# Routed experts as passes of four 32-column strips, 96 places an expert

## What is computed

```python
def moe(h, router_w, router_b, w1, w3, w2):          # h: 384 tokens x 1024
    scores = sigmoid(t @ router_w)                   # 16 experts in 4 groups
    ...                                              # best group, then its two best experts
    combine = sum(one_hot(e_idx, 16) * wts[..., None], axis=1)
    hid = silu(einsum('td,edf->tef', t, w1)) * einsum('td,edf->tef', t, w3)   # f = 256
    hid = hid * combine[:, :, None]
    return einsum('tef,efd->td', hid, w2)
```

## Time and profile before

| | |
|---|---|
| median of 3 runs | 921.61 us (921.53 to 923.45) |
| span of the profiled execution, first to last instruction | 919.5 us |
| TensorE matmul busy | 808.5 us, 88% |
| VectorE / ScalarE / GpSimd busy | 247.2 / 186.0 / 45.9 us |
| moved by DMA | 229.29 MB, mean 249 GB/s |
| chain that ended last | TensorE 81%, DMA 9%, VectorE 5% |
| mean granted TensorE clock | 0.940 of 2.4 GHz |

### The profile page before, as it was taken

How to read it: one execution, slowest core, us unless ns; L and a number is a source line. 1 busy time by engine, 2 the same in 40 slices (tenths; PEclk the granted TensorE clock), 3 DMA queues, 4 the chain that set the end, 5 groups by cost and what they waited for, 6 DMA issues and landing times.

```text
span 919.5 us, 9967 instructions
## 1 busy us (share of the span) xinstructions
PE 808.5 (88%) x4024; PEld 451.8 (49%) x4024; DVE 247.2 (27%) x560; ACT 186.0 (20%) x369; POOL 45.9 (5%) x61
## 2 busy tenths in 40 slices
PE   4699999898986999999992699999769999999914
PEld 2455555575555444444442444565444444444403
DVE  1214035542255112111112510141471121111115
ACT  3100002542041211111111321201231111111112
POOL 1000000000001000000001000000011000000020
PEclk9799999999997999999996799999878999999967
DMA  9953303493365999999878823333337999999151
GB/s 376 429 235 144 115 22 137 179 395 166 138 268 195 377 371 378 371 369 367 345 276 302 332 91 119 137 138 131 144 114 320 354 370 369 372 371 357 46 184 70
DMA packets 23376, 229.29 MB, mean 249 GB/s; under 512 B 2688, under 2 KB 4512, under 8 KB 15520
## 3 DMA queue, kind: packets, MB, share of 16 engines
q1 hardware_dynamic: 9072, 182.06, 50.2%
q0 software_dynamic: 6336, 23.07, 7.1%
q10 hardware_dynamic: 7920, 23.48, 6.4%
HBM read 206.96 MB, written 21.64 MB: 249 GB/s over the span
## 4 chain that ended last, share of the span: by engine, by line
PE 81%; DMA 9%; DVE 5%; issue 2%; ACT 2%; SPq 0%; POOL 0%; ACTq 0%; POOLq 0%; DVEq 0%
PE bank L1418 24%; PE bank L1165 23%; PE bank L1387 12%; PE bank L1493 5%; DMA ring<-in_ev_in 4%; PE bank L1204 2%; PE bank L1401 2%; DMA y_slots<-work 2%; PE bank L1105 2%; DMA work<-y_slots,index 2%; PE bank L1405 2%; PE bank L1136 1%; DVE work L706 1%; PE bank L1297 1%; DVE rstd L732 1%
## 5 line engine op out<-in xcount | busy, mean ns | idle before, releaser
L1418 PE MATMUL bank<-ring,work 128*128 128x512 f32 x512 | 233.5, 600 | 0.0
L1418 PEld LDWEIGHTS bank<-ring,work 128*128 128x128 f32 x512 | 96.1, 193 | 108.7 <-issue 108.7
L1165 PE MATMUL bank<-hT,ring 128*128 128x384 f32 x416 | 136.4, 491 | 3.5 <-DMA ring<-in_ev_in 3.5
L1387 PE MATMUL bank<-ring,work 128*128 128x512 f32 x256 | 115.3, 593 | 2.8 <-ACT work L587 2.8
L1165 PEld LDWEIGHTS bank<-hT,ring 128*128 128x128 f32 x416 | 79.8, 192 | 59.6 <-DMA ring<-in_ev_in 3.7
L1165 PE MATMUL bank<-work,ring 128*128 128x384 f32 x256 | 83.3, 487 | 0.3 <-DVE work L706 0.3
L981 DVE COPY work<-bank 128x512 f32<-128x512 f32 x32 | 22.1, 692 | 214.7 <-PE bank L1405 214.7
L1387 PEld LDWEIGHTS bank<-ring,work 128*128 128x128 f32 x256 | 46.4, 190 | 50.1 <-issue 46.8
L390 POOL DMA_INDIRECT work<-h_all,table x32 | 31.7, 991 | 747.4 <-issue 298.2
L1165 PEld LDWEIGHTS bank<-work,ring 128*128 128x128 f32 x256 | 48.4, 190 | 34.8 <-DVE work L706 1.3
L465 ACT ACTIVATE sq<-xT 128x384 f32<-128x384 f32 x40 | 20.6, 522 | 128.0 <-DVE xT L709 115.5
(11 more groups left out here) (158 smaller groups left out, 642.5 us busy)
## 6 DMA issues: line engine op xcount, KB each, us to landing
ring<-in_moe SPq DMA_DIRECT2D x32, 3072.0 KB, 12.2
ring<-in_ada_w SPq DMA_DIRECT2D x16, 3072.0 KB, 11.1
y_slots<-work ACTq DMA_DIRECT2D x32, 512.0 KB, 11.2
ring<-in_ev_in SPq DMA_DIRECT2D x3, 3072.0 KB, 27.6
ring<-in_gm_in SPq DMA_DIRECT2D x4, 2048.0 KB, 19.1
ring<-in_ev_out SPq DMA_DIRECT2D x2, 2048.0 KB, 10.3
ring<-in_gm_out SPq DMA_DIRECT2D x2, 2048.0 KB, 8.1
h_all<-work ACTq DMA_DIRECT2D x6, 512.0 KB, 5.0
```

The costliest lines, as they stand in the source:

```text
L1165: mm = pe.matmul(ps[:, 0:T], w[:, k, j * P:j * P + P], x[:, k, :], start=(k == 0), stop=(k == KD - 1))
L1387: mm = pe.matmul(ps[half][:, :], hiddenT[:, b, c * P:c * P + P], ring[:, s, at_:at_ + 512], start=(c == 0), stop=(c == 1))
L1418: mm = pe.matmul(bank[e % 2][:, :], h_slotT[:, e % 2, k * P:k * P + P], ring[:, s, k * 512:k * 512 + 512], start=(k == 0), stop=(k == KD - 1))
```

## The change

Experts have 96 places (`CAP`) instead of 128, so that four experts fill three tiles, and 16 experts twelve passes. Of a pass's 128 rows, each block of 32 belongs to one expert (`block_experts`): 0, 0, 0, 1 in pass 0, then 1, 1, 2, 2, then 2, 3, 3, 3, and so on by fours. Each matmul of `up` and `down` becomes four, one per block: 32 stationary columns and that block's expert's weights streaming, into partitions 32n to 32n + 31 of the bank. `up(p)` waits for the chunks of all experts in its blocks. `down(p)` raises `s_expert` by the number of experts that are complete with pass p (`experts_done`): 1, 2, 4 after passes 0, 1, 2, then 5, 6, 8. The ring, its four slots and `load_experts` stay as they are. The engines' loops over rounds are written out. The branch to the routed path asks for at most 96 tokens. The table has three columns for four experts, `fetch` runs twelve times a layer, `y_slots` has 1536 rows, and all six gathers wait for the last store.

The diff, cut to its core (the loops of ScalarE and VectorE change in the same way):

```diff
+CAP = 96
+BLOCK = 32
+PASSES = NE * CAP // P
+TURNS = SLOTS * CAP // P
...
+def block_experts(p):
+
+    return [(p * P + BLOCK * b) // CAP for b in range(P // BLOCK)]
+
+
+def experts_done(p):
+
+    return (p + 1) * P // CAP
...
-        chosen = work[:, chosen_at:chosen_at + NT * NE * P // 2].bitcast(mybir.dt.float16)\
-            .rearrange("p (g t j n) -> p g t j n", g=NE // SLOTS, t=NT, j=SLOTS)
+        chosen = work[:, chosen_at:chosen_at + NT * NE * CAP // 2].bitcast(mybir.dt.float16)\
+            .rearrange("p (g t n) -> p g t n", g=NE // SLOTS, t=NT)
...
-        y_slots = nc.dram_tensor("y_slots", [NE * P, D], F32).ap()
+        y_slots = nc.dram_tensor("y_slots", [PASSES * P, D], F32).ap()
...
-                stored = 16 * NE // 2
                 pool.wait_ge(s_index, l + 1)
-                pool.wait_ge(s_yst[l][0], stored)
-                pool.wait_ge(s_yst[l][1], stored - 16)
+                for b in range(2):
+                    pool.wait_ge(s_yst[l][b], 16 * PASSES // 2)
                 for c, dst in ((0, moe_out), (1, second)):
-                    if c == 1:
-                        pool.wait_ge(s_yst[l][1], stored)
                     for t in range(NT):
-                        pool.indirect_dma_start(dst[:, t, :], None, y_slots[0:(NE - 1 + c) * P, :],
+                        pool.indirect_dma_start(dst[:, t, :], None, y_slots,
...
-                take(tt(s_slot[:, :], ps[:, 0:NT * NE], expert_base, ALU.add), "slots", l)
+                take(stt(s_slot[:, :], expert_base, CAP / P, ps[:, 0:NT * NE], ALU.mult, ALU.add), "slots", l)
...
-                def up(i, e, tiles):
-
-                    s, turn = (chunk + e) % SLOTS, (chunk + e) // SLOTS
+                def up(p, tiles):
+
                     if 0 in tiles:
-                        pe.wait_ge(ring_full[s], i * 16 + 16 * (turn + 1))
-                        pe.wait_ge(s_copy0[l], i * SLOTS + (e + 1))
-                        wait(pe, s_hid[l], i * SLOTS + (e - 1))
+                        for e in sorted(set(block_experts(p))):
+                            pe.wait_ge(ring_full[(chunk + e) % SLOTS], 16 * ((chunk + e) // SLOTS + 1))
+                        pe.wait_ge(s_copy0[l], p + 1)
+                        wait(pe, s_hid[l], p - 1)
                     if 4 in tiles:
-                        pe.wait_ge(s_copy1[l], i * SLOTS + (e + 1))
+                        pe.wait_ge(s_copy1[l], p + 1)
                     for k in tiles:
-                        mm = pe.matmul(bank[e % 2][:, :], h_slotT[:, e % 2, k * P:k * P + P],
-                                       ring[:, s, k * 512:k * 512 + 512], start=(k == 0), stop=(k == KD - 1))
+                        for n, e in enumerate(block_experts(p)):
+                            rows = slice(BLOCK * n, BLOCK * n + BLOCK)
+                            mm = pe.matmul(bank[p % 2][rows, :], h_slotT[:, p % 2, k * P + BLOCK * n:k * P + BLOCK * n + BLOCK],
+                                           ring[:, (chunk + e) % SLOTS, k * 512:k * 512 + 512],
+                                           start=(k == 0), stop=(k == KD - 1))
                     if KD - 1 in tiles:
                         mm.then_inc(s_up[l], 1)
 
-                turn_h(0, 0)
-                up(0, 0, range(KD // 2))
-                turn_h(0, 1)
-                up(0, 0, range(KD // 2, KD))
-
-                def round_(i, static):
-                    for j in range(SLOTS):
-                        b = j % 2
-                        last = static and i > 0
-                        more = not (last and j == SLOTS - 1)
-                        if more:
-                            up(i, j + 1, range(KD // 2))
-                        pe.wait_ge(s_hid[l], i * SLOTS + (j + 1))
+                def down(p):
+
+                    for half in range(2):
                         for c in range(2):
-                            tr = pe.transpose(bank[6 + b][:, c * P:c * P + P], hidden[:, b, c * P:c * P + P], ident[:, :])
-                        tr.then_inc(s_tr[l], 1)
-                        if more:
-                            up(i, j + 1, range(KD // 2, KD))
-                        if not (last and j >= SLOTS - 2):
-                            turn_h(i, j + 2)
-                        pe.wait_ge(s_ht[l], i * SLOTS + (j + 1))
-                        wait(pe, s_y0[l], i * SLOTS + j)
-                        wait(pe, s_y1[l], i * SLOTS + j)
-                        down_matmuls(bank[4:6], b, (chunk + j) % SLOTS).then_inc(s_expert[l], 1)
-
-                rounds(pe, round_)
+                            at_ = KD * 2 * F + c * D + half * 512
+                            for n, e in enumerate(block_experts(p)):
+                                rows = slice(BLOCK * n, BLOCK * n + BLOCK)
+                                mm = pe.matmul(bank[4 + half][rows, :],
+                                               hiddenT[:, p % 2, c * P + BLOCK * n:c * P + BLOCK * n + BLOCK],
+                                               ring[:, (chunk + e) % SLOTS, at_:at_ + 512], start=(c == 0), stop=(c == 1))
+                    mm.then_inc(s_expert[l], experts_done(p) - (experts_done(p - 1) if p > 0 else 0))
+
+                turn_h(0)
+                up(0, range(KD // 2))
+                turn_h(1)
+                up(0, range(KD // 2, KD))
+
+                for p in range(PASSES):
+                    b = p % 2
+                    if p + 1 < PASSES:
+                        up(p + 1, range(KD // 2))
+                    pe.wait_ge(s_hid[l], p + 1)
+                    for c in range(2):
+                        tr = pe.transpose(bank[6 + b][:, c * P:c * P + P], hidden[:, b, c * P:c * P + P], ident[:, :])
+                    tr.then_inc(s_tr[l], 1)
+                    if p + 1 < PASSES:
+                        up(p + 1, range(KD // 2, KD))
+                    if p + 2 < PASSES:
+                        turn_h(p + 2)
+                    pe.wait_ge(s_ht[l], p + 1)
+                    wait(pe, s_y0[l], p)
+                    wait(pe, s_y1[l], p)
+                    down(p)
```

More of the change, by code:

```diff
@@ L310, in wait @@
                 eng.wait_ge(s, value)
[L312 to L318, removed]
         block = ctx.enter_context(nc.Block())
@@ L411, in _ @@
                 count = pool.value_load(most_i[0:1, l:l + 1], min_val=0, max_val=T)
[L412 to L416, removed]
+                with pool.If(count < CAP + 1):
+                    for p in range(PASSES):
+                        fetch(l, p)
+                        if p in (2, 3):
+                            sent(l, p - 2)
                     gather(l)
@@ L925, in place @@
                     own = three(s_tmp)[:, :, g * SLOTS:g * SLOTS + SLOTS].rearrange("p t (j a) -> p t j a", a=1)
-                    tt(chosen[:, g, :, :, :], places, own.to_broadcast([P, NT, SLOTS, P]), ALU.is_equal)\
+                    tt(chosen[:, g, :, :].rearrange("p t (j n) -> p t j n", n=CAP), places,
+                       own.to_broadcast([P, NT, SLOTS, CAP]), ALU.is_equal)\
                         .then_inc(s_chosen, 1)
@@ new lines, in copy_h, with gate @@
+            def copy_h(l, p):
+                dve.wait_ge(s_turn1[l], p + 1)
+                dve.tensor_copy(h_slotT[:, p % 2, 512:D], bank[3][:, :]).then_inc(s_copy1[l], 1)
+            def gate(l, p):
+                dve.wait_ge(s_silu[l], p + 1)
+                tt(hidden[:, p % 2, :], silu[:, p % 2, :], bank[p % 2][:, F:2 * F], ALU.mult).then_inc(s_hid[l], 1)
+            def experts_routed(l):
+                for p in range(2):
+                    copy_h(l, p)
+                gate(l, 0)
+                for p in range(PASSES):
+                    b = p % 2
+                    if p + 2 < PASSES:
+                        copy_h(l, p + 2)
+                    if p + 1 < PASSES:
+                        gate(l, p + 1)
+                    dve.wait_ge(s_expert[l], experts_done(p))
+                    if p >= 2:
+                        dve.wait_ge(s_yst[l][b], 16 * (p // 2))
+                    dve.tensor_copy(y_slot[:, b, 512:D], bank[5][:, :]).then_inc(s_y1[l], 1)
+                    if p == TURNS - 1:
+                        index_rows(l)
@@ L1023, in moe @@
                 steps = chain[0]
-                with dve.If(count < P + 1):
+                with dve.If(count < CAP + 1):
                     experts_routed(l)
@@ L1330, in dispatch @@
                     ps = opened("table", l, g)
-                    for j in range(SLOTS):
+                    for j in range(TURNS):
                         for t in range(NT):
-                            mm = pe.matmul(ps[:, j:j + 1], chosen[:, g, t, j, :], token_h[:, t:t + 1],
+                            mm = pe.matmul(ps[:, j:j + 1], chosen[:, g, t, j * P:j * P + P], token_h[:, t:t + 1],
                                            start=(t == 0), stop=(t == NT - 1))
@@ L1402, in turn_h @@
                     tr.then_inc(s_turn0[l], 1)
-                    wait(pe, s_copy1[l], i * SLOTS + e)
```

(1 more changed line is left out.)

116 lines of the change are left out of this document (45 added, 71 removed).

## The result

The changed kernel takes 1032.9 us (median of 4 runs, 1028.4 to 1037.1) against 921.6; the ratio is 1.120, with an interval from 1.116 to 1.124. It is slower by 12%, where 10% was forecast; 1016 was the value and 986 to 1058 the range.

What follows compares the result with a forecast made beforehand. TensorE, in the routed experts' matmuls, was taken as the bound, with DMA nearly full. Terms -79.8 + 166.8 + 5.6 - 1 + 3 = +94.6 on 919.5 gave 1014.1, plus 2.1 for the runs' median: 1016 us, range 986 to 1058.

Steps and rivals of the forecast that it cites:

- The mechanism: Ring of four slots: up in passes 3, 4, 6, 7, 9, 10 waits for a whole load; 166.8 us with low clock.
- fewer, longer passes: Routed experts: twelve passes of 11.91 us replace sixteen of 11.4, saving 39.9 us a layer, 79.8 in both.
- twelve waits: At up, six waits a layer for a whole expert load, 11.3 us each, ends 10.0 and 14.1.
- low clock behind them: TensorE's granted clock falls in each wait, so matmuls behind it take double for a while: 2.6 us lost each.
- pass 1: up(1) needs expert 2, whose load lands late: +2.7 us in the first layer, +2.9 in the second.
- table and places: Before the experts: smaller comparison of places and three fewer table matmuls, -0.5 us a layer.
- tails: Behind the experts: six gathers after the last store, 0.1 to 3.75 us a layer, taken as +3 in both together.
- Strips: In up and down: four strips run beside each other, 0.11 us lost a pass in rounds, 0.4 in array-strip changes.
- Rival B: Strip weight loads can't run under that strip's own matmul, a round takes 0.54 us: +61 us, 1077 us; 7%.
- C: Routed branch not taken because more than 96 tokens chose one expert: +730 us, 1650 us; 1%.
- Rival D: Longer code of the unrolled loops arrives late, 1.9 us in each of 22 passes: +42, up to 1058 us; 6%.

Runs made afterwards that it cites:

- the load in two parts: Changed kernel, each expert's load from expert 4 on split: w1 and w3 after the last up reading the slot, w2 after its last down; 884.5 us.
- the hold: GpSimd releases the four following loads only once the six gathers have landed; changed kernel 1028.5 us, with the load in two parts 884.2 us.
- the array kept busy: Changed kernel with 16 matmuls of 384 columns, result unused, ahead of the waiting up in each of 12 places; 1002.9 us.

## Why the prediction was right, and where it was off

**The mechanism** is as forecast: 12 waits at the passes named, none at 5, 8 and 11, two short ones at pass 1. It is shown three times: by taking the loads away (-166.5 us), by making the same waits in the kernel before (+166, one run), and by freeing the slots earlier (884.5 us). Three passes with two waits were to take near 64 us and took 63.6 (344.01 to 407.64). The share of the DMA fell, to 0.66 in the first stretch.

**The terms**, as forecast and as measured (both layers, us):

| term | forecast | measured | from |
|---|---|---|---|
| fewer, longer passes | -79.8 | -78.5 | a pass 11.97, forecast 11.91 |
| twelve waits | +135.6 | +138.6 | the waits of TensorE: 11.55 each |
| low clock behind them | +31.2 | +25 | first halves of up in the chain |
| pass 1 | +5.6 | +10 | 2.6 and 5.7, and 1.8 of low clock |
| table and places | -1 | -1.8 | start of the first up |
| tails | +3 | +15.1 | +16.1 in the first layer, -1.0 in the second |
| sum | +94.6 | +108.4 | spans: +110.4 |

The clock term by the chain: the twelve first halves of up behind a wait take 68.6 us together, against 12 x 3.64 at full clock, so 2.1 us a wait where 2.6 was forecast; the low clock lasted 2.6 to 5.6 us, not 4 to 6. The waits were 0.3 us longer than forecast, on the average; the longest, 13.7 us, is that of up(4) in the second layer, whose load took 13.4 us. It was the first of two, but so it is at every up(4), up(7) and up(10), and the other five took 11.1 to 11.6; what held this one up is open. The 2.0 us between the sum and the spans may be the restart: behind a wait a first half takes 3.64 us in the chain even at full clock, and 3.43 where it follows without a gap, fourteen times. This was not tried by itself.

**Strips**: the sum took 4.5 ns a round and 0.1 us a change; measured are nothing a round and 0.14 a change, by luck nearly the same total (0.57 us a pass for 0.51). The Trainium skill ("TensorE: Matmul & The Clock Gate", Measured speedup vs the span model) has 3.07 for four row strips, with column strips beside them. The stream of column strips here runs at 4.0: eight rounds take 3.43 us, what eight records of the whole array take. Rival B falls by the same rows, and C since the routed branch ran (L1414 is in the trace).

**Rival D**, late code, was argued down by a reading that didn't hold: in the waits the DMA is not idle but 86 to 98% busy. It falls by other rows. Loops written out alone cost nothing, and in the version with the load in two parts, which has the long code of the strips and DMA engines that are 95% busy, TensorE's 10.35 us of idle time in 150 are its five waits at up, to the last hundredth. Behind the experts, where code may still be the cause of a halt, D had no term.

**The step that failed** is the tail of the first layer: I costed the six gathers at +3 us and nothing else. Of the 16.1 us there, 4.3 lie between the last down and the issue of the last gather (16.6 us, before 12.3), 4.6 in that gather's landing (14.3 against 9.7), 0.4 in the longer halt behind it, 4.2 in the transposes of the sum, which now halt for 3.1 us in their middle (8.8 us from the first to the last, before 4.6), 1.0 in the mean of squares and 1.7 in the first matmuls of the gated MLP. The late gather alone gave 4 us in both layers. The late load that slows the last store is argued from the issue times alone. A halt of 3.1 to 4.4 us in the first layer's transposes is in five of the six kernels with 96 places (in the changed kernel, without the loads, with the load in two parts, and in both with the hold). The sixth, with the array kept busy, has none there: its 24 transposes take 4.57 us in one piece. None of the kernels made from the one before has it in the first layer, neither with strips nor with loops written out; in the second layer the kernel before halts for 1.0 us itself. So 96 places alone don't make it. The added matmuls change the length of the code and where the transposes stand in it, which fits a cause in the code's place, but nothing was varied for that: the cause stays open. The gains of the second layer's tail show that the gathers by themselves are cheap: its store lands in 2.6 us instead of 6.2.

The pass 1 term was short by 4.5 us. In the second layer the load took 13.1 us, not 11.1 (2.0 us; the one issued at 693.95 had taken 11.7 before, and I took the first layer's lower figure for both), up(1) was ready 0.8 us sooner, and 1.8 us are low clock behind this wait, for which the term had nothing.

## What to carry to other kernels

Packing work so that one pass needs two loads, or one load serves parts of two passes, changes when a buffer comes free: before counting the matmuls saved, write down for each load which pass frees its slot and which instruction in issue order needs it next. With as many slots as before, two periods of slack became none. A buffer can often be freed in parts; that cost no memory here and turned 12% slower into 4% faster. Where TensorE waits, add the low clock behind the wait, here 2.1 us behind 11.55.

## Not expected of the hardware

- Four strips of 32 columns that stream 512 columns of float32 each ran wholly beside each other: 32 records in 3.43 us, 0.107 us a record, with no loss a round; a change between whole-array and strip work cost 0.14 us each way.
- Useless matmuls in the waits kept the granted clock at full behind ten of twelve of them and gave 20.4 us back in the first halves of up.
- Of two loads of 3 MB issued 0.5 to 0.9 us apart on one queue, the first landed as if it were alone (11.0 us, as single ones did; one took 13.4), and the second after 17.9 to 19.7. An idle TensorE made no load faster: twelve loads issued into its waits took 10.8 to 13.4 us, against 10.9 to 14.6 before.
